# Both directions of a doubling step sent to TensorE together, by all four quarters of its array

## The reference

```python
def wkv_scan(state0, r, kk, v, decay, b, k, reverse):
    def step(S, inp):
        r_t, kk_t, v_t, w_t, b_t, k_t = inp
        sa = jnp.einsum('bhij,bhj->bhi', S, kk_t)
        S = S * w_t[:, :, None, :] - sa[..., None] * b_t[:, :, None, :] + v_t[..., None] * k_t[:, :, None, :]
        return S, jnp.einsum('bhij,bhj->bhi', S, r_t)
    return lax.scan(step, state0, (r, kk, v, decay, b, k), reverse=reverse)
...
    for d, reverse in enumerate((False, True)):
        ctx_state, y_c = wkv_scan(state0, *c_common, *c_dirs[d], reverse=reverse)
        _, y_l = wkv_scan(ctx_state, *l_common, *l_dirs[d], reverse=reverse)
```

## Time and profile before

| | |
|---|---|
| time, median of 3 (lowest to highest) | 2142.56 us (2142.12 to 2144.69) |
| the profiled execution: time, span | 2142.36 us, 2140.6 us |
| TensorE matmul, busy | 1955.3 us, 91% of the span |
| TensorE weight loads, busy | 1738.9 us, 81% |
| the chain that ended last, by engine | PE 69%, DVE 13%, DMA 4%, ACT 4% |
| VectorE, ScalarE, GpSimd busy | 1408.8, 1042.2, 390.9 us |
| mean granted TensorE clock | 0.966 of full |
| the stage of recurrence and attention | about 985 to 1191 us of the span |

### The profile page before, as it was taken

One profiled execution on the slowest core, in us unless ns is written; L12 is line 12 of the kernel. 1 busy time (PEld: TensorE's weight loads), 2 busy tenths in 40 slices (PEclk: granted clock), 3 DMA queues, 4 the chain that ended last, 5 costly groups with the idle time before them and its releaser, 6 DMA issues.

```text
span 2140.6 us, 40342 instructions
## 1 busy us (share of the span) xinstructions
PE 1955.3 (91%) x15183; PEld 1738.9 (81%) x15183; DVE 1408.8 (66%) x2268; ACT 1042.2 (49%) x2078; POOL 390.9 (18%) x330
## 2 busy tenths in 40 slices
PE   6998899978889998998889769999999999999996
PEld 6875788868878887997667669899899998777775
DVE  5545578766867676235544558888799986666665
ACT  4343434446845344333444334444677775555554
POOL 2101000000100000000000003787666670000000
PEclk9999999999999999997999979999999999999998
DMA  7542566653465785331000553555554445556553
GB/s 268 183 173 87 197 206 228 234 198 121 156 217 177 258 273 176 128 114 13 2 3 7 153 120 93 153 161 161 155 142 142 141 139 177 188 193 187 188 192 129
DMA packets 212576, 333.54 MB, mean 156 GB/s; under 512 B 23494, under 2 KB 140860, under 8 KB 212424
## 3 DMA queue, kind: packets, MB, share of 16 engines
q1 hardware_dynamic: 208888, 320.06, 47.1%
q0 software_dynamic: 3536, 11.34, 1.6%
HBM read 330.26 MB, written 1.08 MB: 155 GB/s over the span
## 4 chain that ended last, share of the span: by engine, by line
PE 69%; DVE 13%; DMA 4%; ACT 4%; issue 4%; PEld 2%; SPq 2%; PEldq 0%; POOL 0%; DVEq 0%; ACTq 0%
PE psum L2328 20%; PE psum L2329 19%; PE psum L2330 19%; PE psum L2931 3%; DVE u_turned L2231 2%; DMA u_rows<-in_peer_u_dram 2%; DVE weights_lo L1571 2%; SPq L942 1%; PE psum L2766 1%; PE psum L2755 1%; ACT weights_hi L1090 1%; PE psum L2760 1%; PE psum L2638 1%; PEld psum L2328 1%; PEld psum L2329 1%
## 5 line engine op out<-in xcount | busy, mean ns | idle before, releaser
L1571 DVE TENSOR_TENSOR weights_lo<-weights,weights_hi 128x1024 fp32r<-128x1024 f32 (+2 forms) x336 | 345.5, 1086 | 273.4 <-ACT weights_hi L1090 268.5
L2328 PE MATMUL psum<-input_hi,weights_hi 128*128 128x256 f32 x1288 | 371.9, 289 | 14.1 <-DVE input_lo L1598 5.1
L1090 ACT ACTIVATE weights_hi<-weights 128x1024 fp32r<-128x1024 f32 (+2 forms) x336 | 289.2, 931 | 178.7 <-PEq L2375 117.9
L1069 POOL TENSOR_TENSOR u_lo<-u_turned,u_hi 128x512 fp32r<-128x512 f32 x256 | 330.6, 1314 | 214.8 <-ACT u_hi L1468 214.7
L2329 PE MATMUL psum<-input_lo,weights_hi 128*128 128x256 f32 x1288 | 367.7, 285 | 0.0
L2330 PE MATMUL psum<-input_hi,weights_lo 128*128 128x256 f32 x1288 | 367.2, 285 | 0.0
L2328 PE MATMUL psum<-input_hi,u_hi 128*128 128x256 f32 x1024 | 298.3, 291 | 13.1 <-POOL u_lo L1069 12.1
L2329 PE MATMUL psum<-input_lo,u_hi 128*128 128x256 f32 x1024 | 291.6, 285 | 0.0
L2330 PE MATMUL psum<-input_hi,u_lo 128*128 128x256 f32 x1024 | 291.5, 285 | 0.0
L2328 PEld LDWEIGHTS psum<-input_hi,weights_hi 128*128 128x128 f32 x1288 | 250.6, 195 | 29.6 <-issue 27.8
L2329 PEld LDWEIGHTS psum<-input_lo,weights_hi 128*128 128x128 f32 x1288 | 250.8, 195 | 0.0
(11 more groups left out here) (386 smaller groups left out, 3660.2 us busy)
## 6 DMA issues: line engine op xcount, KB each, us to landing
u_rows<-in_peer_u_dram SPq DMA_DIRECT2D x512, 128.0 KB, 2.6
weights<-in_ffn_w_in_dram SPq DMA_DIRECT2D x44, 1024.0 KB, 7.3
v_rows_even<-in_peer_v_dram SPq DMA_DIRECT2D x64, 512.0 KB, 3.5
v_rows_odd<-in_peer_v_dram SPq DMA_DIRECT2D x64, 512.0 KB, 3.5
weights<-in_ret_w_in_dram SPq DMA_DIRECT2D x24, 1024.0 KB, 7.4
ada_rows_in<-in_ada_w_dram SPq DMA_DIRECT2D x24, 1024.0 KB, 5.2
weights<-in_ffn_w_out_dram SPq DMA_DIRECT2D x44, 512.0 KB, 6.3
weights<-in_lru_w_in_dram SPq DMA_DIRECT2D x12, 1024.0 KB, 6.4
```

The source lines that it names most:

```text
L1069: nc.gpsimd.tensor_tensor(UTL[:, b, half, :], turned[:, half, :], UTH[:, b, half, :].bitcast(F32), ALU.subtract).then_inc(s_ul[b], 1)
L1090: nc.scalar.activation(whi[:, r, at_], wraw[:, r, at_], ACT.Copy).then_inc(s_whi[r], 1)
L1571: ins = nc.vector.tensor_tensor(wlo[:, r, at_], wraw[:, r, at_], whi[:, r, at_].bitcast(F32), ALU.subtract)
L2328: nc.tensor.matmul(o, ah, bh, start=start, stop=False)
```

## The change

Three edits. First, t, y and xy (`LOCKED`) of both directions are issued together at the item of d = 1; the products of d = 1 go by the two off-diagonal quarters. For that, t and y of d = 1 write the other half of the partitions (`there`), and xy reads from there and writes back to its own. Each direction keeps its own bank. Second, attention and other side work is held back by `mixed_plan` until it stands before an item that is not the second of a pair. Third, the wait of VectorE for the copies of ab is counted in the order in which they are made.

```diff
+LOCKED = ("t", "y", "xy")
...
+    waiting = []
     for at_, item in enumerate(rwkv_plan()):
-        for what, i in sorted(beside.get(at_, []), key=lambda x: x[1]):
-            yield None, None, None, what, i
-        if at_ in OTHER_WORK:
-            yield (None, None, None, *OTHER_WORK[at_])
+        waiting += sorted(beside.get(at_, []), key=lambda x: x[1]) + [OTHER_WORK[x] for x in (at_,) if x in OTHER_WORK]
+        _, d, _, what, n = item
+        if not (what in LOCKED and d == 1 or what in PAIRED and n == 1):
+            yield from ((None, None, None, *w) for w in waiting)
+            waiting = []
         yield item
...
-                    dve.wait_ge(s_aa, 4 * k + 2 * n + d + 1)
+                    dve.wait_ge(s_aa, 4 * k + 2 * d + n + 1)
...
+                if what in LOCKED:
+                    of_both = lambda what, n: [UNITS["rwkv"] + RW_UNIT[k, e, what, n] for e in range(2)]
+                    banks = [free_bank(v) for v in of_both(what, n)]
+                    if what == "t":
+                        for v in (of_both("xy", n - 1) if n > 1 else of_both("lev", 0)):
+                            evacuated(v)
+                    elif what == "y":
+                        pe.wait_ge(s_am, 12 * k + (4 if n == 1 else 2 * n + 2))
+                    else:
+                        for v in of_both("t", n) + of_both("y", n):
+                            evacuated(v)
+                    for j in range(4):
+                        for e in range(2):
+                            for c in range(2):
+                                here, there = slice(64 * c, 64 * c + 64), slice(64 * (c ^ e), 64 * (c ^ e) + 64)
+                                if what == "t":
+                                    left, right, to = XX[e][here, j // 2, j % 2, :], SQM[here, 16, :], there
+                                elif what == "y":
+                                    left, right, to = (AM[e][here, n % 2, j // 2, j % 2, :], XX[e][here, j // 2, j % 2, :],
+                                                       there)
+                                else:
+                                    left, right, to = TI[e][there, j // 2, j % 2, :], YY[e][there, j // 2, j % 2, :], here
+                                ins = nc.tensor.matmul(PS[to, banks[e], j * 64:j * 64 + 64], left, right, start=True, stop=True)
+                                if (j, c) == (3, 1):
+                                    ins.then_inc(s_full[banks[e]], 1)
                     continue
```

More of the change, by code:

```diff
@@ L272, in mixed_plan @@
                 beside[NA_FIRST + NA_APART * i + later].append(("ny", i // 8))
+    waiting = []
     for at_, item in enumerate(rwkv_plan()):
-        for what, i in sorted(beside.get(at_, []), key=lambda x: x[1]):
-            yield None, None, None, what, i
-        if at_ in OTHER_WORK:
-            yield (None, None, None, *OTHER_WORK[at_])
+        waiting += sorted(beside.get(at_, []), key=lambda x: x[1]) + [OTHER_WORK[x] for x in (at_,) if x in OTHER_WORK]
[3 more added lines that the diff above has]
+            waiting = []
         yield item
-    assert max(beside) <= at_
+    assert max(beside) <= at_ and not waiting
 PEER_UNITS = [("q", 0), ("q", 1), *[("k", n) for n in range(4)], ("q", 2), ("s", 0), ("s", 1), ("q", 3),
@@ L2702, in _ @@
                     continue
-                if what in PAIRED and n == 0:
+                if what in PAIRED and n == 0 or what in LOCKED and d == 0:
+                    continue
+                if what in LOCKED:
[23 more added lines that the diff above has]
+                                    ins.then_inc(s_full[banks[e]], 1)
                     continue
@@ L2751, in _ @@
                                                SQM[ch_, 16, :], start=True, stop=True)
[L2752 to L2767, removed]
                 elif what == "ug":
```

## The result

| | before | changed |
|---|---|---|
| median (lowest to highest), 11 runs each | 2144.21 us (2140.24 to 2147.45) | 2155.03 us (2148.03 to 2159.01) |
| ratio | | 1.0049, 95% interval 1.0037 to 1.0061 |
| mean granted clock, profiled execution | 0.966 | 0.953 |
| us at the low clock between 985 and 1190, added up from windows of 1 us | 14.5, all before 1000 | 68.5 |

The change makes the kernel slower, by some 10.8 us. I forecast 4.7 us faster, and my rival with this cause came to no change. The page of the changed kernel shows TensorE's busy time hardly lower (1948.2 us against 1955.3), although 60 pairs were to take half. That is the first hint.

A forecast was written before the change was run, and what follows sets the result against it. The stage was taken as nearly bound by TensorE, with ScalarE's copies and the ring of four banks close behind. Gains of 4.0 + 0.7 = 4.7 us off 2142.36 gave 2137.7 us, range 2131 to 2149.

The forecast's parts named there:

- my rival with this cause: Recurrence and attention stage: idle TensorE has its clock lowered or raised later; 2141 us, no change that can be told; 10%.
- the second rival: Recurrence and attention stage: TensorE's clock drops, or rises later at the start, costing some 3 us; 2141 us; 10%.
- the 2.65 that kept it at full speed: Stage before the change: one 5 us window had 2.65 us of matmul and the clock stayed at 1.00.
- The quarters overlap four at a time: Pairs of t, y and xy: full rate assumed, 0.62 us with tail, saving 0.46 us a pair.
- The circle of a locked step: Doubling step, t through copies, y, xy and subtractions to next t: 3.72 us with nothing between, longer with attention.
- The sum of the stage: Steps of the four chunks, walked with attention in place: together 4.0 us gained.
- the walk: Hand count of the doubling steps in the engines' queue order, mean step 4.95 us.
- The other edits, +0.7: Wait at ab, attention moved out of pairs, first step's wait: bounded between -0.7 and +1.4 us, taken as +0.7 gain.
- The first rival: Every pair: quarters do not overlap four at a time, pair stays 0.93 us; 26 us more, about 2164 us; 13%.

The follow-up runs named there:

- experiment 5: Changed kernel with one useless TensorE product, not three, behind each y and xy that no attention follows: 2145.10 us, ratio 1.0008.
- experiment 4: Changed kernel with three useless TensorE products behind each y and xy that no attention follows: 2137.88 us, ratio 0.9980.
- experiment 1: Changed kernel with the second direction's products on the same two diagonal quarters as the first's: 2167.06 us, ratio 1.0103.
- experiment 2: Kernel before with the changed plan and the corrected wait at ab, each direction's items issued singly: 2134.16 us, ratio 0.9959.
- experiment 8: Three kernels with useless products at the stage's start; the one cited is the changed kernel with only y by four quarters: 2131.90 us, ratio 0.9944.

## Why the prediction was wrong

Its failed step is one sentence, in the second rival: "With 3.1 us of work in a 5 us step the stage stays well above the 2.65 that kept it at full speed." It failed twice over. The 3.1 us were a mean over a step, and the changed kernel has emptier stretches: TensorE was busy 2.22 of the 5 us ahead of the fall at 1108.72. And the one window of before was no bound: ahead of the falls at 1047.28 and 1060.94 TensorE was busy 3.10 and 2.89 us, more than 2.65, and the clock fell all the same, while it stayed at 1.00 through 5 us with 1.75. What the runs showed in place of a clock that stays up is 60.8 us at 0.50 between 1000 and 1190 us, where the kernel before had none. I had the right mechanism as a rival, priced it for the start alone (3 us, no change), and gave it 10%. The whole stage took 54 us more at the low clock, some 18 us by experiment 5, and holding the clock up in experiment 4 gave 15 to 17 back.

Point by point:

- *The quarters overlap four at a time*: right. A pair lasts 0.69 with its tail; I said 0.62 with it. Both row halves write one bank at once. The rule that different row tiles cannot access one PSUM bank at the same time (the Trainium skill: TensorEngine Tiling (Array Packing), Restrictions and Gotchas) made no difference here: 32 instructions take 0.69 us, and the same 32 on the two diagonal quarters take 1.15 (experiment 1).
- *The circle of a locked step*: right where the clock was full, within 0.05 us at every point of the step shown.
- *The sum of the stage*: too low by hand. With the filling, the inverses of chunks 2, 3 and 4 took 26.1, 28.0 and 24.5 us from t to ug, where I had 25.0, 25.6 and 23.0; before, from its first t, they took 26.7, 26.2 and 25.2. Chunks 2 and 4 ran wholly at full clock there, so that the walk was short by 1.1 and 1.5 us, and the pairing with the new plan gains 0.6 a chunk on before. Against the same plan with single items (experiment 2: 26.6 and 24.7) it gains 0.5 and 0.2, and 1.9 in chunk 1 (25.2 against 27.0), but its first t begins 2.6 later (992.45 against 989.90). Chunk 3 is 1.8 longer than before, with 6.8 us of it at the low clock, some 2.3 us by experiment 5. So at full clock the pairing itself gains little here.
- *The other edits, +0.7*: too small. The wait at ab and the plan are worth 8.8 us together (ratio 0.9959). In the profile most of it is there by the end of the first inverse, which TensorE begins earlier and at full clock. That experiment 4 came out at 2137.88, a fifth of a microsecond from my forecast, is thus chance: two errors of opposite sign.
- *The first rival* (no overlap) was wrong as a fact, but its price, 26 us over the forecast, is near what experiment 1 shows, which is that case: 29 us by the medians over the filled pairs, 26 by the ratios, of which some 7 come by its 22 us more of low clock.

In all: 1.0049 is 0.9959 for the plan and the wait, times 1.0090 for the pairing, about 19 us. The pairing adds 65 us at the low clock (68.5 against the 3.4 of experiment 2), some 22 us by experiment 5. So the clock accounts for all of the loss, within what these runs can tell.

Open: what exactly makes the clock fall. The runs with an emptier TensorE tend to have more low clock, but its busy time as the profile counts it does not settle the matter. Between 1000 and 1190 us it was busy 156.8 us in experiment 8 with y alone paired, and 6.8 us were low; it was busy 157.4 in experiment 5 and 162.3 in experiment 4, and 30.7 and 13.7 were low. Nor does one idle spell settle it: the 1.51 us ahead of 1070.37 brought no fall. Nor is it shown whether the earlier rise in experiment 2 comes from a denser start or from a shift by a microsecond.

## What to carry to other kernels

Work taken off TensorE in a stage full of short waits can be paid back at half clock: look at the granted clock first, and price a fall over the whole stage, not over its start. The fastest kernels here pair only y, which adds no wait but that for its bank, and leave t and xy apart on different quarters; that this beats single items is not shown, their intervals overlap. When an edit touches a wait, time that wait alone: here the two small edits were the gain and the large one the loss.

## What was not expected of the hardware

- Useless products on TensorE made the changed kernel some 15 to 17 us faster (2155.03 to 2137.88), with 13.8 us at the low clock instead of 68.5.
- The clock fell behind stretches with 2.22, 2.89 and 3.10 of 5 us busy, and stayed at 1.00 through one with 1.75 of the same run and one with 2.65 of before.
- Items of two directions issued one after the other on different quarters take 0.97 us where both on the diagonal take 1.15.
- One program (experiment 5) scattered over 20 us with its mean clock, where the 11 runs of the kernel before spread over 7.
